# Delta rule of a hybrid decoder layer: the state meets the raw keys, and the triangular inverse is applied to the remainder

## What is computed

```python
t_inv = inverse(eye + strict_lower((k * beta) @ k.T * decay))      # 64 x 64
u = t_inv @ (v * beta)
w = t_inv @ (k * beta * exp(g))
qk = q @ k.T * decay

def step(S, inp):                        # chunk after chunk, S is 128 x 128
    v_new = u_c - w_c @ S
    o = (q_c * exp(g_c)) @ S + qk_c @ v_new
    S = S * exp(g_last) + (k_c * exp(g_last - g_c)).T @ v_new
    return S, o
```

## Time and profile before

| | us |
|---|---|
| median of 3 runs (2991.09 to 2991.76) | 2991.72 |
| span of the profiled execution | 2990.1 |
| TensorE busy in it | 2817.9 (94%) |
| VectorE, ScalarE, GpSimd busy | 1814.3, 1181.2, 1144.1 |
| delta stage: its first `first(1)`, and the first matmul of the stage behind it | at 708.7, at 1022.4 |

### The profile page before, as it was taken

The page is one execution under the profiler, slowest core; times in us unless marked ns, Lnnn a source line. Parts: engine busy times, 40 slices in busy tenths (PEclk is TensorE's granted clock), DMA queues, the critical chain, the costliest instruction groups (busy, mean ns, idle before and its releaser), DMA issues. The chain is left out here.

```text
span 2990.1 us, 48834 instructions
## 1 busy us (share of the span) xinstructions
PE 2817.9 (94%) x18995; PEld 2440.4 (82%) x18995; DVE 1814.3 (61%) x2759; ACT 1181.2 (40%) x2210; POOL 1144.1 (38%) x1213
## 2 busy tenths in 40 slices
PE   7998979997999899998999599999999999999999
PEld 7997779996888688887788478888788888788887
DVE  3226834443555587777796677777887777543544
ACT  3226722223545365555443433333433333332321
POOL 2535930004776200001553456666666666100000
PEclk9999989997999899999999799999999999999999
DMA  8975953225454022221575633333533333654554
GB/s 269 354 251 171 263 166 111 67 74 130 108 147 87 22 75 91 85 68 40 179 246 164 216 93 105 95 103 94 190 105 99 101 105 97 240 170 146 192 167 142
DMA packets 403278, 421.07 MB, mean 141 GB/s; under 512 B 34075, under 2 KB 325995, under 8 KB 401000
## 3 DMA queue, kind: packets, MB, share of 16 engines
q1 hardware_dynamic: 368400, 298.61, 33.5%
q10 hardware_dynamic: 19944, 66.63, 6.8%
q0 software_dynamic: 14704, 52.69, 5.4%
HBM read 257.51 MB, written 160.34 MB: 140 GB/s over the span
## 5 line engine op out<-in xcount | busy, mean ns | idle before, releaser
L3526 PE MATMUL fu_pM<-fu_us_hi,fu_w_ring 128*128 128x512 f32 x2464 | 772.6, 393 | 15.2 <-DVE fu_us_lo L3361 14.3
L3526 PEld LDWEIGHTS fu_pM<-fu_us_hi,fu_w_ring 128*128 128x128 f32 x2464 | 466.3, 189 | 120.5 <-DVE fu_us_lo L3361 17.0
L3526 PE MATMUL fu_pM<-fu_us_lo,fu_w_ring 128*128 128x512 f32 x1232 | 482.8, 392 | 0.0
L3526 PEld LDWEIGHTS fu_pM<-fu_us_lo,fu_w_ring 128*128 128x128 f32 x1232 | 233.4, 189 | 47.8
L3262 ACT ACTIVATE fu_w_ring<-fu_sw 128x512 fp32r<-128x512 f32 x176 | 110.9, 631 | 325.3 <-PE fu_pM L3526 264.1
L3368 DVE TENSOR_TENSOR fu_w_ring<-fu_sw,fu_w_ring 128x512 fp32r<-128x512 f32 x132 | 139.4, 1056 | 65.4 <-ACT fu_w_ring L3262 65.3
L3368 DVE TENSOR_TENSOR fu_w_ring<-fu_w_raw,fu_w_ring 128x512 fp32r<-128x512 f32 x88 | 108.5, 1233 | 104.3 <-ACT fu_w_ring L3262 104.3
L2995 PE MATMUL fu_pM<-fu_us_hi,fu_w_ring 128*128 128x512 f32 x666 | 169.3, 391 | 1.3 <-DVE fu_w_ring L2918 1.3
L3262 ACT ACTIVATE fu_w_ring<-fu_w_raw 128x512 fp32r<-128x512 f32 x132 | 83.0, 629 | 191.3 <-PE fu_pM L3526 169.9
L3409 DVE SCALAR_TENSOR_TENSOR fu_acc<-fu_gb,fu_taps,fu_acc 128x1024 f32<-128x1024 f32 x88 | 133.0, 1513 | 37.7 <-ACT fu_acc L3303 36.9
L2075 ACT ACTIVATE at_pt_hi<-at_pT 128x512 fp32r<-128x512 f32 (+3 forms) x176 | 92.7, 539 | 143.6 <-PE at_pT L2340 142.7
(11 more groups left out here) (539 smaller groups left out, 7141.5 us busy)
## 6 DMA issues: line engine op xcount, KB each, us to landing
fu_w_ring<-scr_gs ACTq DMA_DIRECT2D x37, 704.0 KB, 4.6
fu_w_raw<-in_w_gate SPq DMA_DIRECT2D x22, 1024.0 KB, 5.4
fu_w_raw<-in_w_up SPq DMA_DIRECT2D x22, 1024.0 KB, 5.4
scr_gs<-fu_sg SPq DMA_DIRECT2D x84, 256.0 KB, 3.0
scr_gs<-fu_acc SPq DMA_DIRECT2D x63, 256.0 KB, 2.9
fu_us_lo<-scr_gs ACTq DMA_DIRECT2D x19, 704.0 KB, 4.6
pj_wd<-in_w_down POOLq DMA_DIRECT2D x11, 1024.0 KB, 9.3
scr_td<-pj_td POOLq DMA_DIRECT2D x11, 1024.0 KB, 8.0
```

The lines of the kernel that those rows point to most:

```text
L3526: p = pe.matmul(bank(2 * n + m, i)[:, :], a[:, k, :], x[:, k, :], start=(k == 0 and n_pass == 0), stop=(k == HALVES_K - 1 and n_pass == 2))
```

## The change

W and the scaled keys `kbg` are no longer made. Instead of v_new = U - W S the kernel computes v_new = T (v beta - f (K S)), with T the inverse and f the row factor `kscale`. `predict(c)` multiplies the raw keys by the state (as soon as the state is there, without the inverse); VectorE's `remainder(c)` multiplies by the row factor and subtracts `vb`; TensorE's `solve(c)` applies the inverse; the sign is put into the inverse at its last level; ScalarE's `values(c)` copies the result out of PSUM. `final`, `u_part` and `w_part` go, and the orders of the three lists are new. `load` waits also for `ws[1]` of the tile whose keys lie in the buffer; `scale` and ScalarE's `strict` wait for `rest_made[1]`.

```diff
@@ sync, load
                     sp.wait_ge(late_ready[(t - LOADS) % 2], (t - LOADS) // 2 + 1)
                     sp.wait_ge(kk[(t - LOADS) % 2], (t - LOADS) // 2 + 1)
+                    sp.wait_ge(ws[1], t - LOADS + 1)
@@ gpsimd, scale
-                pool.wait_ge(u_done[s], 2 * u)
-                pool.wait_ge(w_done[s], u)
+                if t > 1:
+                    pool.wait_ge(rest_made[1], t - 1)
...
-                pool.wait_ge(kscale_ready[s], u + 1)
-                pool.tensor_tensor(kbg[s][:, :, :].rearrange("p (c g) d -> p c g d", c=2), kv[t % LOADS][:, :, 0:2, :],
...
@@ scalar
             def strict(t, s, u):
                 act.wait_ge(small_ready[s], u + 1)
-                act.wait_ge(scaled[s], u)
+                if t > 1:
+                    act.wait_ge(rest_made[1], t - 1)
                 act.activation(kscale[s][:, :], scs[s][:, 0, :], ACT.Exp).then_inc(kscale_ready[s], 1)
...
+            def values(c):
+                def run(t, s, u):
+                    act.wait_ge(solved[c], t + 1)
+                    act.wait_ge(o_done[c], t)
+                    act.activation(vn[c][:, :, :], pN, ACT.Copy).then_inc(v_ready[c], 1)
+                return run
+            plain(DT, (0, level(1)), (-1, values(0)), (1, strict), (0, level(2)), (0, level(3)), (-1, out(0)), (-1, values(1)),
+                  (0, level(4)), (1, turned), (2, square), (1, causal), (0, level(5)), (1, row_decay), (-1, out(1)), (2, inverse))
@@ vector
+            def remainder(c):
+                def run(t, s, u):
+                    dve.wait_ge(scaled[s], u + 1)
+                    dve.wait_ge(kscale_ready[s], u + 1)
                     dve.wait_ge(ws[c], t + 1)
+                    dve.wait_ge(solved[c], t)
+                    for gg in range(2):
+                        un = 2 * c + gg
+                        o = dve.scalar_tensor_tensor(out=rest[c][:, gg, :], in0=pV[:, gg, :], scalar=kscale[s][:, un:un + 1],
+                                                     in1=vb[s][:, un, :], op0=ALU.mult, op1=ALU.subtract)
+                    o.then_inc(rest_made[c], 1)
+                return run
...
+            plain(DT, (-1, remainder(0)), (0, level(1)), (-1, state(0)), (-1, remainder(1)), (0, level(2)), (1, strict),
+                  (0, level(3)), (0, level(4)), (-1, state(1)), (0, level(5)), (2, square_sums), (1, attention))
@@ tensor, predict
-                            m = pe.matmul(pV[rows, gg, :], wt[s][:, hh, 2 * c + gg, :], st[c][:, 2 * gg + hh, :],
+                            m = pe.matmul(pV[rows, gg, :], kqT[t % LOADS][:, 2 * gg + hh, cols], st[c][:, 2 * gg + hh, :],
...
+            def solve(c):
+                def run(t, s, u):
+                    pe.wait_ge(x_step[c], STEPS * (t + 1))
+                    pe.wait_ge(rest_made[c], t + 1)
+                    pe.wait_ge(v_ready[1 - c], t + c)
+                    for gg in range(2):
+                        for rows in HALVES:
+                            m = pe.matmul(pN[rows, gg, :], xx[s][rows, 2 * c + gg, 1, :], rest[c][rows, gg, :], start=True, stop=True)
+                    m.then_inc(solved[c], 1)
+                return run
...
+            plain(DT, (-1, predict(0)), (0, first(1)), (-1, solve(0)), (0, second(1)), (-1, update(0)), (0, first(2)),
+                  (-1, outputs(0)), (-1, predict(1)), (0, second(2)), (0, first(3)), (-1, solve(1)), (1, products), (0, second(3)),
+                  (0, first(4)), (-1, update(1)), (0, second(4)), (1, turn), (0, first(5)), (-1, outputs(1)), (0, second(5)),
+                  (2, q_norm))
```

More of the change, by code:

```diff
@@ L1365, in stage_delta @@
         egr = r.sb("egr", [P, UNITS, P])
-        kbg = [r.sb(f"kbg{i}", [P, UNITS, P]) for i in range(2)]
         vb = [r.sb(f"vb{i}", [P, UNITS, P]) for i in range(2)]
@@ L1374, in stage_delta @@
         kd = [r.sb(f"kd{i}", [P, UNITS, P]) for i in range(2)]
-        wt = [r.sb(f"wt{i}", [P, 2, UNITS, C2]) for i in range(2)]
-        uu = [r.sb(f"uu{i}", [P, UNITS, P]) for i in range(2)]
+        rest = [r.sb(f"rest{i}", [P, 2, P]) for i in range(2)]
         st = [r.sb(f"st{i}", [P, HEADS, P]) for i in range(2)]
@@ L1383, in stage_delta @@
         pS = [r.ps(f"pS{i}", [P, 4, P]) for i in range(2)]
-        pU = r.ps("pU", [P, UNITS, P])
+        pU = r.ps("pU", [P, 4, P])
         pW = r.ps("pW", [P, 512])
@@ L1388, in stage_delta @@
         pO, pV = pU[:, 0:2, :], pW[:, 0:2 * P].rearrange("p (g n) -> p g n", g=2)
+        pN = pW[:, 2 * P:4 * P].rearrange("p (g n) -> p g n", g=2)
         state_clear, loaded = r.sem("state_clear"), [S["dn_loaded0"]] + r.sems("loaded", LOADS - 1)
@@ L1397, in stage_delta @@
         p_done, p_out, q_done, x_step = (r.sems(x) for x in ("p_done", "p_out", "q_done", "x_step"))
-        u_done, w_done, u_out, w_out = (r.sems(x) for x in ("u_done", "w_done", "u_out", "w_out"))
+        rest_made, solved = (r.sems(x) for x in ("rest_made", "solved"))
         ws, v_ready, ks, s_ready, o_done, o_out, stored = (
@@ L1507, in scale @@
                                    scs[s][:, 1, :].rearrange("p (c g) -> p c g", c=2).unsqueeze(3).to_broadcast([P, 2, 2, P]),
-                                   ALU.mult)
-                pool.wait_ge(kscale_ready[s], u + 1)
-                pool.tensor_tensor(kbg[s][:, :, :].rearrange("p (c g) d -> p c g d", c=2), kv[t % LOADS][:, :, 0:2, :],
-                                   kscale[s][:, :].rearrange("p (c g) -> p c g", c=2).unsqueeze(3).to_broadcast([P, 2, 2, P]),
                                    ALU.mult).then_inc(scaled[s], 1)
@@ L1640, in run @@
                             x, q = x[:, :, 1, :], q[:, :, 1, :]
-                        dve.tensor_tensor(x, q, x, ALU.add).then_inc(x_step[c], 1)
-                return run
[L1644 to L1648, removed]
+                            dve.scalar_tensor_tensor(out=x, in0=q, scalar=-1.0, in1=x, op0=ALU.mult,
+                                                     op1=ALU.subtract).then_inc(x_step[c], 1)
+                        else:
+                            dve.tensor_tensor(x, q, x, ALU.add).then_inc(x_step[c], 1)
+                return run
+            def remainder(c):
                 def run(t, s, u):
-                    if c == 0:
-                        dve.wait_ge(u_out[s], u + 1)
+                    dve.wait_ge(scaled[s], u + 1)
+                    dve.wait_ge(kscale_ready[s], u + 1)
                     dve.wait_ge(ws[c], t + 1)
-                    dve.wait_ge(o_done[c], t)
-                    dve.tensor_tensor(vn[c][:, :, :], uu[s][:, 2 * c:2 * c + 2, :], pV, ALU.subtract).then_inc(v_ready[c], 1)
+                    dve.wait_ge(solved[c], t)
[4 more added lines that the diff above has]
+                    o.then_inc(rest_made[c], 1)
                 return run
@@ L1672, in state @@
                 return run
-            plain(DT, (-1, values(0)), (0, level(1)), (-1, state(0)), (0, level(2)), (1, strict), (0, level(3)),
-                  (-1, values(1)), (0, level(4)), (-1, state(1)), (0, level(5)), (2, square_sums), (1, attention), (0, u_part))
+            plain(DT, (-1, remainder(0)), (0, level(1)), (-1, state(0)), (-1, remainder(1)), (0, level(2)), (1, strict),
+                  (0, level(3)), (0, level(4)), (-1, state(1)), (0, level(5)), (2, square_sums), (1, attention))
         @block.tensor
@@ L1741, in second @@
                 return run
[L1743 to L1757, removed]
             def predict(c):
@@ L1761, in run @@
                     if c == 0:
-                        pe.wait_ge(w_out[s], u + 1)
+                        pe.wait_ge(loaded[t % LOADS], 128 * (t // LOADS + 1))
                         pe.wait_ge(s_ready[1], t)
-                        pe.wait_ge(v_ready[1], t)
+                        pe.wait_ge(rest_made[1], t)
                     else:
                         pe.wait_ge(s_ready[0], t + 1)
-                        pe.wait_ge(v_ready[0], t + 1)
+                        pe.wait_ge(rest_made[0], t + 1)
+                    cols = slice(c * CHUNK, c * CHUNK + CHUNK)
                     for gg in range(2):
                         for hh, rows in enumerate(HALVES):
-                            m = pe.matmul(pV[rows, gg, :], wt[s][:, hh, 2 * c + gg, :], st[c][:, 2 * gg + hh, :],
+                            m = pe.matmul(pV[rows, gg, :], kqT[t % LOADS][:, 2 * gg + hh, cols], st[c][:, 2 * gg + hh, :],
                                           start=True, stop=True)
                     m.then_inc(ws[c], 1)
+                return run
[8 more added lines that the diff above has]
+                    m.then_inc(solved[c], 1)
                 return run
@@ L1803, in outputs @@
                 return run
-            plain(DT, (0, first(1)), (-1, predict(0)), (0, second(1)), (0, first(2)), (-1, update(0)), (0, second(2)),
-                  (1, products), (0, first(3)), (-1, outputs(0)), (0, second(3)), (-1, predict(1)), (0, first(4)), (1, turn),
```

(5 more changed lines are left out.)

## The result

The changed kernel takes 3081.86 us (median of 4 runs, 3077.82 to 3083.15) against 2991.74 us; the ratio is 1.0302 (95% interval 1.0287 to 1.0316), so it is slower by 90 us. The forecast was 3082. The profiled execution has a span of 3076.0 us, 85.9 more than before.

What follows compares the result with a forecast made beforehand. The prediction took TensorE's in-order queue to bound the delta stage. 2991.7 us plus 77 for new waits net of removed work gave 3069; 13 for the clock gave 3082, range 3040 to 3108.

Steps and rivals of the forecast that it cites:

- TensorE's queue is the bound: Delta stage: TensorE's in-order queue sets the time; removed matmuls shorten it, each moment it waits lengthens it.
- floor of 15.93: TensorE work per delta-stage step: 17.57 less 1.04 us of W matmuls and 0.60 us of old stalls.
- First wait: Before `second(2)`: ScalarE's `level(2)` copy is queued behind `strict`, which waits for chunk 1's remainder; TensorE waits 2.29 us.
- Second wait: Before `update(1)`: stores queued behind the later load delay ScalarE's `out(0)` and `values(1)`; stall 2.9 us (2.5 to 3.4).
- Third wait: Before the last `second`: squares and decay on ScalarE delay the `level(5)` copy; stall 1.19 us.
- the walk: One delta-stage step followed block by block: 15.93 us of work plus 7.35 of new stalls, 23.3 us, without clock change.
- the term for the clock: Slower TensorE clock after stalls in the delta stage: 1.0 us per step (0 to 3.4), 13 us in all.
- Rival (a): TensorE's clock stays full in the delta stage, as in the skill's rule: 3069 us; chance 0.22.
- Rival (b): Stores land early enough or SyncE issues faster, so only ScalarE's wait bites: 3044 us; chance 0.18.
- Rival (c): TensorE's clock falls twice per step without cover, 13 x 2.4 us more: 3113 us; chance 0.12.
- Rival (d): `strict` or `out(0)` is not late, TensorE stays filled, the removed block is the whole effect: 2974 us; chance 0.04.
- The covered load: Loads land near T 15.5; the GpSimd work they delay is needed about T 24, covered with little over 1 us.

Runs made afterwards that it cites:

- three_factors: Changed kernel with three buffers instead of two for the row factors, so ScalarE's `strict` waits for nothing of its own step: 3089.54 us, ratio 1.0335.
- level5_early: `both_four_buffers` with ScalarE's `level(5)` moved ahead of `square` and `causal`: 2979.70 us, ratio 0.9953.
- stores_first: Changed kernel with the two stores ahead of the load in SyncE's list: 3061.48 us, ratio 1.0242.
- stores_first_filled: `stores_first` with 28 matmuls that nobody reads put between `predict(1)` and `second(2)`: 3037.56 us, ratio 1.0151.
- both: Changed kernel with stores ahead of the load and three row-factor buffers: 3041.02 us, ratio 1.0170.
- four_filled: `both_four_buffers` with 12 matmuls that nobody reads put between `outputs(1)` and `second(5)`: 2998.19 us, ratio 1.0021.
- both_four_buffers: `both` with four load buffers instead of three: 3007.55 us, ratio 1.0060.
- new_order: `both_four_buffers` with TensorE's list reordered so another block stands in each gap but one, ScalarE and VectorE following: 2973.41 us, ratio 0.9933.

## Why the prediction was right

**TensorE's queue is the bound.** Right: 0.42 us less waiting before `solve(0)` showed as 0.42 us less per step, down to 16.10 us against a floor of 15.93. Against the kernel before that is 1.45 us less, W's 1.04 us of matmuls and most of its 0.6 us of stalls.

**First wait, `strict` behind the remainder.** Predicted 2.29 us, measured 29.8 / 13 = 2.29. Its place and its releaser are as told. But the experiment adds something that the prediction's sum, which lists it as a cost of its own, did not say: removed alone, it is worth nothing (`three_factors`), as the second wait takes its place.

**Second wait, stores behind the load.** Right in mechanism: SyncE's queue waits for `predict(1)` in all thirteen steps, the output copy for a store in all thirteen. Predicted: `update(1)` starts at T 16.75 in place of 13.84. Measured in the step shown: 885.91 - 868.89 = 17.02. The issues of the load take 4.99 us (875.18 to 880.17) where I took 5.45. The output copy starts 4.8 us after the first store's issue, and 3.6 to 5.0 in the thirteen steps (mean 4.5), where I took 4.1. `predict(1)` starts 5.54 us into the step; I had 5.36. These errors nearly cancel. The idle time that the rows show there is only 16.4 / 13 = 1.26 us, not 2.9, because the blocks before it run at the lower clock. I had said that a fall between the first two waits costs nothing for this reason.

**Third wait.** Predicted 1.19, and `level5_early` gave back 1.17. The profile's idle row says 0.95, as the durations of matmuls overlap; from start to start `outputs(1)` takes 2.20 us (888.61 to 890.81) where the block alone was priced at 1.08, which leaves 1.12.

**The sum and the clock.** The trace tells the two apart. In seven of the thirteen steps `predict(1)` starts 5.54 us into the step. The other six begin at the lower clock, and there it starts at 6.54 to 6.78: 6.8 us in all. One more step loses 0.4 us behind `update(1)`. Every step also has a slow stretch behind the first wait, which the store wait covers. So the clock cost 7.2 us in thirteen steps, 0.55 us per step, and the step without it is 23.77 - 0.55 = 23.22 us against the 23.3 of the walk. The walk was right; the term for the clock, 1.0 us per step and 13 us in all, was too high by nearly a half. Without its slow stretches `stores_first` takes 20.55 (`stores_first_filled`), so the store wait itself is 23.22 - 20.55 = 2.7 us, predicted 2.9.

What made up for the clock's term is partly chance. The steps around the thirteen cost 5 us in place of 3. The median of the runs lies 4 us above the run that was profiled (3077.82), and of that the forecast knew nothing; the kernel before itself varied by 9 us in a later comparison (2985.5 to 2994.4), so these 4 us ask for no cause. The hit to 0.2 us is luck; the terms are good to some 10 us.

**Rival (a), the clock stays full,** falls: it is 0.89 over thirteen steps, and the filled kernels show what that can cost. By the Trainium skill's TensorE: Matmul & The Clock Gate, section Why this matters for your kernels, gaps of 0.95 and 2.29 us should not have closed the gate. This case does not agree: the rows at 879 and 805 show the clock at 0.50 behind them, and with the gaps filled it stayed at 1.00. Here each gap had other short waits or the one-column matmuls of `q_norm` near it, and no run tells what a single such gap would do. **Rival (b)** falls by the 57.2 us of waiting for stores and by the 20 us that `stores_first` gave back. **Rival (c)** did not happen: no step had two uncovered stretches, six had one, and the others have the store wait to cover theirs but for the 0.4 us above. **Rival (d),** faster, needs other orders and buffers than the change has: the versions at 2966 to 2980 are what it described.

**The covered load.** The late load was rightly costed at nothing here, but with "little over 1 us" to spare; `both`, with shorter steps, ran out of that cover, and four buffers in place of three gave back 33 us.

## What to carry to other kernels

When matmuls are taken off the engine that is the bound, ask which buffers are now read for longer, and what stands queued behind the wait that protects each: here a wait on a load held back unrelated stores, and one on a small vector held back the copies that the next matmuls needed. Of the two long waits in a row on this path only the later one paid when removed alone; removing the earlier only moved its idle time. Price TensorE's idle time twice, once as itself and once for the slower clock behind it, unless another wait covers the slow stretch.

## What the runs showed of the hardware

Matmuls whose result nobody reads made a kernel faster by 0.8% (`stores_first_filled`) and 0.3% (`four_filled`), with the granted clock at 1.00 in the steps. In `both_four_buffers` a gap of 0.95 us beside the 1 us of one-column matmuls of `q_norm` was enough for a stretch at 0.50 in every other step. In `new_order`, with a gap of 0.75 us in every step and the rest of the step dense, the clock stayed at 1.00 from 724.6 to 956.6 us, fourteen steps. What the one-column matmuls have to do with it was not tested. Two stores issued right behind eight load transfers were down 3.6 to 5.0 us after the first one's issue in the changed kernel; all stores in this stage of the kernel before landed in 2.0 to 4.6 us, with a median of 2.1.
